# Expert stream of a fused attention, mixture-of-experts and HGRN layer: its first late piece and its last piece in two halves, its spare piece earlier, and a fourth pair of split-weight buffers in the second block

## The chip, the cores and the metric

One core of a Trainium2 chip runs the whole program. The metric is the device time of one execution in microseconds (us), median of several executions. TensorE is called PE below, VectorE DVE, ScalarE ACT, GpSimd POOL and SyncE SP; SP does nothing but wait on semaphores and issue transfers.

## The reference

The input is 256 tokens of width 1024 in float32. The first block is attention with a relative bias, a layer norm, and a mixture of 32 experts of which each token takes 4. The second block is an HGRN2 and convolution mixer and a gated feed-forward net of width 2816. The part around the change is the end of the first norm, the experts and the norm behind them, and then the matrix products of the second block.

```python
h = layer_norm(DEEPNORM_ALPHA * h + t, ln_g[i, 0], ln_b[i, 0])
f = moe_ffn(h, ...)
h = layer_norm(DEEPNORM_ALPHA * h + f, ln_g[i, 1], ln_b[i, 1])
...
logits = (xt @ w_router + b_router).astype(jnp.float32)
top_logit, top_e = lax.top_k(logits, TOP_K)
gate = jax.nn.softmax(top_logit, axis=-1)
...
def expert_block(args):
    h = xb @ w_gu[e] + b_gu[e]
    h_gate, h_up = jnp.split(h, 2, axis=-1)
    h_gate = jnp.minimum(h_gate, SWIGLU_LIMIT)
    h_up = jnp.clip(h_up, -SWIGLU_LIMIT, SWIGLU_LIMIT)
    act = h_gate * jax.nn.sigmoid(SWIGLU_ALPHA * h_gate) * (h_up + 1.0)
    return act @ w_down[e] + b_down[e]
```

## The kernel before

**The expert stream.** All weights of all 32 experts are read from HBM: per expert four pieces of `w_gu` and two of `w_down`, 2 MB each, 192 pieces numbered 0 to 191. They go to a ring of ten slots in SBUF; piece 10 (`SPARE`) alone has a place outside it, in the arena at 8192. Piece n of 11 and above goes to slot (n-1) mod 10, and SP issues its transfer (`load_piece`, L489) when `freed(n)` holds, which is that PE has finished with the piece that was in that slot: piece 11 waits for piece 0, piece 12 for piece 1, piece 15 for piece 4, piece 21 for piece 11, piece 22 for piece 12. The experts run in order, except that at the end the gate and up pieces of expert 31 come ahead of the down pieces of expert 30. So the last four pieces are 188 and 189 (down of expert 30) and 190 and 191 (down of expert 31).

**One expert on PE.** The tokens of the expert are gathered (L808, up to 64 of them), turned (L624), copied by ACT, multiplied with four gate and up pieces (L835), the result is clipped and gated on DVE and ACT, turned, multiplied with two down pieces (L843) and added to the sums of all tokens (`scatter`, L855). The bias of the expert is put into the accumulators first (`add_bias`, L827).

**Ahead of the stream.** Attention's output product (L751) ends tile by tile; DVE forms the sum, its norm with the rows `ln_g` and `ln_b` (`row_g`, `row_b`, arena 8192 to 10240) and so `h1`. PE turns `h1`, multiplies it with the router's weights (L790), DVE picks four experts a token (`choose`), PE counts the place of each token in its expert's list (L797 to L801), DVE makes the selection matrices, PE gathers. PE then makes three small tables of gates, places and counts (L624, L867), before the first expert starts. Since `row_g` and `row_b` lie where piece 10 goes, SP issues piece 10 only after `h1` of both tiles is done.

**Loads by POOL.** The rows of the first norm are loaded after the last row maximum, the small arrays of the router and of the gate biases after the last attention values; `bdown` and the rows of the second norm after piece 10 has been used.

**After the stream.** The last down result goes through ACT (`take_items`) and `scatter`, DVE and ACT form the norm of both tiles and the RMS norm of the second block. Its weights come in 1 MB pieces to six places in slots 3 to 5 (L545). ACT splits each piece into a high part (`split_hi`, L1198) and DVE into a low part (`split_lo`, L1552), in one of three pairs of buffers in slots 6 to 8 (`w_split`), and PE makes three products of them. The wait of `split_hi` is for PE to be done with the piece three before. In the last product (L1143) all accumulators are fed together for eight pieces, and then the last three are used once for each accumulator. Slot 9 is not used after the stream.

## Time and profile before

| | us |
|---|---|
| median of 3 runs | 1375.93 (1375.58 to 1377.43) |
| the profiled execution | 1376.69 |
| its span in the trace | 1374.9 |
| granted clock of PE, mean | 0.994 of full speed |
| attention and first norm, to the first expert product | 0 to 132.3 |
| expert stream, to the last down product | 132.3 to 1033.2 |
| second norm and second block | 1033.2 to 1374.9 |

The busy share of an engine says little here: PE counts as busy in 97% of the span, in all stages. What bounds a stage is read from what PE waits for in it, and from the rate of the transfers.

### The profile page before, as it was taken

The page shows a single profiled execution, that of the slowest core. Times are in us where ns is not written, and L with a number is a line of the kernel's source. Part 1 is how long each engine was busy: PE and PEld are TensorE (multiplying, and loading weights), DVE is VectorE, ACT ScalarE, POOL GpSimd, SP SyncE. Part 2 cuts the span into 40 slices and gives each one's busy share as a digit, 9 for nine tenths or more (in the row PEclk, how much of TensorE's full clock was granted, in tenths as well). Part 3 has the DMA queues.
Part 4 walks back from the last instruction along what each step waited for, and adds up shares of the span by engine and source line. Part 5 has one row for each costly group of instructions (what it writes and reads, how often), then busy time and mean ns, then how long its engine had stood idle before and what let it go on. Part 6 is the DMA issues. An engine that isn't in the chain of part 4 may idle for free.

```text
span 1374.9 us, 17056 instructions
## 1 busy us (share of the span) xinstructions
PE 1330.1 (97%) x7358; PEld 718.6 (52%) x7358; DVE 441.2 (32%) x746; ACT 346.9 (25%) x576; POOL 49.6 (4%) x60
## 2 busy tenths in 40 slices
PE   9999999999999999969999999999999999999997
PEld 7996333333333333323333333333336998999986
DVE  5565121112111111101211111111107776888854
ACT  4541011101101110100110101100116545666642
POOL 2010000000000000000000000000002000022200
PEclk9999999999999999989999999999999999999999
DMA  9968999999999999999999999999996444265530
GB/s 378 376 233 359 428 421 430 430 432 429 430 431 430 430 431 429 431 429 430 431 432 429 432 429 431 429 431 430 432 427 242 153 154 153 87 254 183 184 123 31
DMA packets 44378, 484.17 MB, mean 352 GB/s; under 512 B 4780, under 2 KB 4832, under 8 KB 13712
## 3 DMA queue, kind: packets, MB, share of 16 engines
q1 hardware_dynamic: 42432, 477.63, 83.4%
q0 software_dynamic: 1872, 5.44, 1.1%
q8 instruction: 59, 0.97, 0.3%
q14 instruction: 15, 0.12, 0.0%
HBM read 481.99 MB, written 1.06 MB: 351 GB/s over the span
## 4 chain that ended last, share of the span: by engine, by line
PE 78%; DMA 15%; DVE 4%; issue 1%; ACT 1%; DVEq 0%; SPq 0%; ACTq 0%
PE bank L835 25%; PE bank L641 19%; PE bank L843 13%; DMA ring<-in_moe_w_gate_up 12%; PE bank L1143 4%; PE bank L855 3%; PE bank L808 3%; PE bank L624 3%; DMA ring<-in_w_in 2%; PE bank L827 2%; PE bank L751 2%; PE bank L1079 1%; PE bank L1029 1%; DMA arena<-in_x_by_feature 1%; DVE w_split L1552 1%
## 5 line engine op out<-in xcount | busy, mean ns | idle before, releaser
L835 PE MATMUL bank<-ring,arena 128*64 128x512 f32 x2048 | 448.9, 594 | 9.8 <-DMA ring<-in_moe_w_gate_up 9.8
L835 PEld LDWEIGHTS bank<-ring,arena 128*64 128x64 f32 x2048 | 143.2, 137 | 313.2 <-issue 290.3
L1750 DVE TENSOR_SCALAR arena<-bank 128x512 f32<-128x512 f32 x32 | 22.1, 692 | 654.8 <-PE bank L835 654.7
L843 PE MATMUL bank<-ring,arena 128*64 128x512 f32 x1008 | 223.5, 595 | 1.8 <-DMA ring<-in_moe_w_down 1.3
L641 PE MATMUL bank<-x_hi,w_split 128*128 128x256 f32 x1056 | 195.2, 285 | 2.1 <-DVE x_lo L1559 2.1
L641 PEld LDWEIGHTS bank<-x_hi,w_split 128*128 128x128 f32 x1056 | 167.2, 193 | 2.6 <-DVE x_lo L1559 1.5
L1552 DVE TENSOR_TENSOR w_split<-ring,w_split 128x2048 fp32r<-128x2048 f32 x61 | 139.5, 2289 | 60.4 <-ACT w_split L1198 60.2
L641 PE MATMUL bank<-x_lo,w_split 128*128 128x256 f32 x528 | 150.1, 284 | 0.0
L1299 ACT ACTIVATE arena<-arena 128x512 f32<-128x512 f32 x32 | 20.2, 630 | 495.3 <-DVE arena L1750 495.3
L843 PEld LDWEIGHTS bank<-ring,arena 128*64 128x64 f32 x1008 | 69.8, 137 | 135.3 <-issue 126.4
L1198 ACT CAST w_split<-ring 128x2048 fp32r<-128x2048 f32 x62 | 118.2, 1910 | 74.2 <-PE bank L641 42.5
L641 PEld LDWEIGHTS bank<-x_lo,w_split 128*128 128x128 f32 x528 | 102.1, 193 | 0.0
L808 PE MATMUL bank<-arena 128*64 128x512 f32 x256 | 61.9, 605 | 10.6 <-issue 10.6
L1291 ACT COPY arena<-bank 128x512 f32<-128x512 f32 x32 | 18.7, 585 | 200.4 <-PE bank L843 200.4
L855 PE MATMUL bank<-arena 64*128 64x512 f32 x256 | 63.6, 615 | 1.5 <-ACT arena L1291 1.5
L624 PEld LDWEIGHTS bank<-cst,arena 128*128 128x128 f32 (+1 forms) x374 | 45.0, 188 | 34.9 <-DVE arena L1758 26.3
L624 PE MATMUL bank<-cst,arena 128*128 128x128 f32 (+1 forms) x374 | 54.4, 290 | 5.4 <-DVE arena L1758 3.3
L1143 PE MATMUL bank<-w_split,a_hi 128*128 128x512 f32 x176 | 54.4, 390 | 1.6 <-DVE w_split L1552 1.6
L2043 DVE SCALAR_TENSOR_TENSOR ring<-ring,vcol 128x256 f32<-128x256 f32 x88 | 48.8, 594 | 1.6 <-ACT ring L1526 0.8
L641 PE MATMUL bank<-w_split,x_hi 128*128 128x256 f32 x256 | 49.0, 287 | 0.0
L855 PEld LDWEIGHTS bank<-arena 64*128 64x128 f32 x256 | 22.0, 186 | 42.1 <-issue 38.6
L808 PEld LDWEIGHTS bank<-arena 128*64 128x64 f32 x256 | 18.4, 139 | 47.7 <-issue 46.9
(288 smaller groups left out, 1102.1 us busy)
## 6 DMA issues: line engine op xcount, KB each, us to landing
ring<-in_moe_w_gate_up SPq DMA_DIRECT2D x128, 2048.0 KB, 34.5
ring<-in_moe_w_down SPq DMA_DIRECT2D x63, 2048.0 KB, 34.1
ring<-in_ffn_w_up SPq DMA_DIRECT2D x22, 1024.0 KB, 4.8
ring<-in_w_in SPq DMA_DIRECT2D x14, 1024.0 KB, 8.0
ring<-in_ffn_w_down SPq DMA_DIRECT2D x11, 1024.0 KB, 4.9
ring<-in_a_w_in SPq DMA_DIRECT2D x10, 1024.0 KB, 20.9
ring<-in_a_w_out SPq DMA_DIRECT2D x2, 2048.0 KB, 14.0
ring<-in_w_out SPq DMA_DIRECT2D x4, 1024.0 KB, 5.0
```

What stands on the lines that cost most here:

```text
L624: return pe.transpose(dst, src, ident[0:rows, 0:rows])
L641: last = mm(dst[:, j * T:(j + 1) * T], lhs, rhs, start=c == 0 and n == 0, stop=c == KC - 1 and n == 2)
L751: last = mm(bank[OUT_BANKS[2 * g + t]][:, :], a, w[:, cols], start=h == 2 * first and k == 0, stop=h == 2 * last_q + 1 and k == 2)
L808: last = mm(bank[2][half * 64:half * 64 + 64, :], sel[:, t, :], h1[:, t, half * 512:(half + 1) * 512], start=t == 0, stop=t == NT - 1)
L827: mm(bank[q][half * 64:half * 64 + 64, :], bias_sel[rows, :], bgu[rows, :], start=True, stop=False)
L835: last = mm(bank[q // 2][half * 64:half * 64 + 64, :], chunk(xeT, c), w[:, c % 2, q * 512:(q + 1) * 512], start=False, stop=c == KC - 1)
L843: last = mm(bank[3][half * 64:half * 64 + 64, :], chunk(actT, c), w[:, c % 4, half * 512:(half + 1) * 512], start=c == 0, stop=c == KC - 1)
L855: last = mm(bank[4 + 2 * half + t][:, :], selgT[rows, t, :], y_item[rows, :], start=first, stop=True, skip_group_check=True)
L1143: last = mm(bank[2 * t + g][:, :], x, w, start=c == 0 and k == 0, stop=c == FB - 1 and k == 2)
L1198: copy(like(w_hi, p), pieces[p][2]).then_inc(hi_ready, 1)
L1552: tt(like(w_lo, p), pieces[p][2], like(w_hi, p).bitcast(f32), ALU.subtract).then_inc(lo_ready, 1)
L2043: last = stt(y[:, g, :], u[:, g, j:j + T], vcol[:, col:col + 1], y[:, g, :], ALU.mult, ALU.add)
```

## The change

1. The rows of the first norm get places of their own (`row_g0` at 13612, loaded early; `row_b0` at 6144, loaded when the attention values are done). Piece 10 is issued right then, ahead of pieces 0, 6, 7 and 8.
2. Piece 11 is loaded in two halves: the first when PE has done the first half of piece 0 (`first_chunk`), the second when it has done all of it.
3. The rows of the second norm are loaded by SP behind piece 191, and no longer by POOL after piece 10.
4. `h1` of each tile is announced in halves. Ranks, places and selection are made tile by tile, and the gather of the first tile runs ahead of the choice for the second. The first expert's bias is added earlier, and the three small tables are made behind piece 0. PE runs short fill products (`fill`) between them.
5. Piece 191 is loaded in halves, and PE uses each when it is there. `scatter(1)` and the turn of the gates of expert 31 move behind piece 190. ACT takes the last result ahead of `split_hi(IN2)`, and loads its table earlier.
6. From `IN2` on there are four pairs of split buffers; the fourth is slot 9. `split_hi` waits for the piece four before. Where ACT and DVE stand in their own order with each split is not changed.

```diff
+        row_g0, row_b0 = at(13612, D), at(6144, D)
...
         def arrived(n):
-            return ring_in[home(n)], 16 * sum(home(k) == home(n) for k in range(n + 1))
+            return ring_in[home(n)], 16 * sum((home(k) == home(n)) * (1 + (k == HALVED[0])) for k in range(n + 1))
+        HALVED = (SPARE + 1, N_EXP * PIECES_E - 1)
+        def split_of(p):
+            return p % SPLITS if p < IN2 else (p - IN2) % LATE_SPLITS
...
+            sp.wait_ge(o_ps, PAIRS)
+            load_piece(SPARE)
             for k, q in enumerate(OUT_ORDER):
                 sp.wait_ge(*((out_used, k + 1) if k < PAIRS - 1 else (out_ps, NT + 1)))
                 load_piece(SPLIT_X if q == SPLITS else SPLIT_FIRST + (OUT1 + q) % SPLITS)
-            sp.wait_ge(h1_ready, NT)
-            load_piece(SPARE)
-            for n in range(SPARE + 1, first_late):
+            sp.wait_ge(first_chunk, 1)
+            load_half(HALVED[0], 0)
+            sp.wait_ge(*freed(HALVED[0]))
+            load_half(HALVED[0], 1)
+            for n in range(SPARE + 2, first_late):
                 sp.wait_ge(*freed(n))
                 load_piece(n)
...
+            sp.wait_ge(*freed(HALVED[1]))
+            for j in range(2):
+                load_half(HALVED[1], j)
+            sp.dma_start(row_g, row(ln_g[1, :], D)).then_inc(ln1_in, 16)
+            sp.dma_start(row_b, row(ln_b[1, :], D)).then_inc(ln1_in, 16)
...
-            pool.wait_ge(max_ready, H)
-            pool.dma_start(row_g, row(ln_g[0, :], D)).then_inc(ln0_in, 16)
-            pool.dma_start(row_b, row(ln_b[0, :], D)).then_inc(ln0_in, 16)
+            pool.dma_start(row_g0, row(ln_g[0, :], D)).then_inc(rel_in, 16)
             pool.wait_ge(pt_ps, H)
             pool.wait_ge(o_ps, PAIRS)
+            pool.dma_start(row_b0, row(ln_b[0, :], D)).then_inc(ln0_in, 16)
...
             pool.dma_start(bdown, b_down[:, :]).then_inc(moe_small_in, 16)
-            pool.dma_start(row_g, row(ln_g[1, :], D)).then_inc(ln1_in, 16)
-            pool.dma_start(row_b, row(ln_b[1, :], D)).then_inc(ln1_in, 16)
...
+            pe.wait_ge(sel_ready, 1)
+            gather_first(0)
+            mm(RANKS[1], ones, chosen[:, 0, :], start=True, stop=False)
+            fill()
             pe.wait_ge(chosen_ready, 2)
-            mm(bank[0][:, N_EXP:2 * N_EXP], before, chosen[:, 1, :], start=False, stop=True).then_inc(rank_ps, 1)
-            repeat(3, 1)
+            mm(RANKS[1], before, chosen[:, 1, :], start=False, stop=True).then_inc(rank_ps, 1)
+            fill()
+            pe.wait_ge(sel_ready, 2)
+            gather_first(1).then_inc(xe_ps, 1)
+            fill()
...
+                    if n == 0:
+                        gate_up(s, buffer_of(n, 2), (0,)).then_inc(first_chunk, 1)
+                        gate_up(s, buffer_of(n, 2), (1,)).then_inc(piece_done, 1)
+                        tables()
...
+                    if n == HALVED[1]:
+                        scatter(1)
+                        pe.wait_ge(selg_ready, i + 1)
+                        turn_gates().then_inc(selgT_ps, 1)
+                        pe.wait_ge(*arrived(n))
+                        down_e(s, buffer_of(n, 4), (0, 1))
+                        pe.wait_ge(last_half_in, 32)
+                        down_e(s, buffer_of(n, 4), (2, 3)).then_inc(piece_done, 1)
...
-                elif p >= DOWN + SPLITS:
-                    act.wait_ge(piece_used, p - DOWN - SPLITS + 1)
+                elif p >= DOWN + LATE_SPLITS:
+                    act.wait_ge(piece_used, p - DOWN - LATE_SPLITS + 1)
...
                 if i == LAST:
-                    split_hi(IN2)
+                    nc.scalar.preload_act_table_set(log_exp)
                 if i != LAST - 1:
                     take_items(i)
+                if i == LAST:
+                    split_hi(IN2)
```

SP's order at the start of the stream, before: `in_moe_w_down` to the arena is piece 10, the ring piece behind it piece 11.

```order
L489 DMA ring<-in_moe_w_gate_up 128x4096
L489 DMA ring<-in_moe_w_down 128x4096
L489 DMA arena<-in_moe_w_down 128x4096
L489 DMA ring<-in_moe_w_down 128x4096
L489 DMA ring<-in_moe_w_gate_up 128x4096 x4
```

And of the change, with its waits at the same place:

```order
L500 DMA ring<-in_moe_w_down 128x4096 [waits lo_ready]
L500 DMA arena<-in_moe_w_down 128x4096 [waits o_ps]
L500 DMA ring<-in_moe_w_gate_up 128x4096 [waits out_used] x3
L500 DMA ring<-in_moe_w_gate_up 128x4096 [waits out_ps]
L510 DMA ring<-in_moe_w_down 128x2048 [waits first_chunk]
L510 DMA ring<-in_moe_w_down 128x2048 [waits piece_done]
L500 DMA ring<-in_moe_w_gate_up 128x4096 [waits piece_done] x4
```

Piece 10 now stands ahead of the four pieces that wait for the output product, and piece 11 is two rows.

PE's order from the ranks of the second tile to the end of the first expert's gate and up product, before (128x32 rows on L797 to L801 are ranks, L808 the gather, L624 turns, L867 counts, L827 the bias, L835 gate and up):

```order
L797 MATMUL bank<-arena,cst 128x32
L798 MATMUL bank<-arena,cst 128x32
L649 MATMUL bank<-cst 128x512
L801 MATMUL bank<-arena,cst 128x32
L649 MATMUL bank<-cst 128x512
L808 MATMUL bank<-arena 64x512 x4
L624 MATMUL bank<-cst,arena 32x128 x4
L867 MATMUL bank<-cst,arena 32x1 x2
L624 MATMUL bank<-cst,arena 128x128 x4
L827 MATMUL bank<-arena 64x512 x4
L835 MATMUL bank<-ring,arena 64x512 x32
```

And of the change, from the gather of the first tile (L814 gathers, L820 is a fill, L881 gate and up):

```order
L814 MATMUL bank<-arena 64x512 x2
L848 MATMUL bank<-arena,cst 128x32
L820 MATMUL bank<-cst 128x256
L851 MATMUL bank<-arena,cst 128x32
L820 MATMUL bank<-cst 128x256
L814 MATMUL bank<-arena 64x512 x2
L820 MATMUL bank<-cst 128x256
L650 MATMUL bank<-cst,arena 128x128 x4
L820 MATMUL bank<-cst 128x256
L881 MATMUL bank<-ring,arena 64x512 x8
L650 MATMUL bank<-cst,arena 32x128 x4
L917 MATMUL bank<-cst,arena 32x1 x2
```

Behind the last rank there is now half a gather where a whole one was, the bias is gone from there (it follows the first tile's router product), and the tables stand behind the eight products of piece 0.

## Rows read from the trace of the kernel before

**Rows 1.** The page: span, and the rate of transfers in 40 slices.
```profile
span 1374.9 us, 17056 instructions
GB/s 378 376 233 359 428 421 430 430 432 429 430 431 430 430 431 429 431 429 430 431 432 429 432 429 431 429 431 430 432 427 242 153 154 153 87 254 183 184 123 31
```
**Rows 2.** PE's waits, 135 to 1047 us: total us, times, longest.
```profile
PE bank L808 <- issue: 10.6, 1, 10.6
PE bank L835 <- DMA ring<-in_moe_w_gate_up: 9.8, 11, 1.5
...
PE bank L843 <- DMA ring<-in_moe_w_down: 1.3, 2, 1.1
```
**Rows 3.** Windows: busy by engine, PE clock, DMA share, GB/s.
```profile
108.00:112.00 4.00, 4.00 (x19) 3.32 (x18) 3.83 (x8) 0.41 (x2) 0.00 (x0) 1.00 0.06 19
200.00:250.00 50.00, 50.00 (x246) 17.40 (x244) 7.10 (x16) 6.30 (x12) 0.00 (x0) 1.00 1.01 430
```
**Rows 4.** Timeline of SP's queue: issues of pieces 11, 12 and 21.
```profile
135.97 0.33 SPq L489 DMA_DIRECT2D ring<-in_moe_w_down  x1
139.41 0.33 SPq L489 DMA_DIRECT2D ring<-in_moe_w_gate_up  x1
...
186.48 0.33 SPq L489 DMA_DIRECT2D ring<-in_moe_w_gate_up  x1
```
**Rows 5.** DMA issues to landing: alone at 77.17, pieces 11, 12, 21, second norm's `ln_b`.
```profile
ring<-in_moe_w_gate_up SPq DMA_DIRECT2D x1, 2048.0 KB, 7.8
...
ring<-in_moe_w_down SPq DMA_DIRECT2D x1, 2048.0 KB, 8.8
...
ring<-in_moe_w_gate_up SPq DMA_DIRECT2D x1, 2048.0 KB, 10.2
...
ring<-in_moe_w_gate_up SPq DMA_DIRECT2D x1, 2048.0 KB, 10.6
...
arena<-in_ln_b POOLq DMA_DIRECT2D x1, 512.0 KB, 13.3
```
**Rows 6.** Timeline, all engines, 127 to 133 us.
```profile
127.96 1.94 PE L808 MATMUL bank<-arena 128*64 128x512 f32 x8
...
129.83 0.61 PE L624 MATMUL bank<-cst,arena 128*32 128x128 f32 x4
...
130.59 0.74 PE L624 MATMUL bank<-cst,arena 128*128 128x128 f32 x4
...
131.26 1.09 PE L827 MATMUL bank<-arena 32*64 32x512 f32 x8
...
131.37 0.58 ACT L1296 COPY arena<-bank 128x512 f32<-128x512 f32 x1 [0.84 <-PE bank L624]
...
132.28 7.95 PE L835 MATMUL bank<-ring,arena 128*64 128x512 f32 x36
```
**Rows 7.** Timeline, all engines, 1019 to 1039 us.
```profile
1019.50 3.65 PE L843 MATMUL bank<-ring,arena 128*64 128x512 f32 x16 [1.09 <-DMA ring<-in_moe_w_down]
...
1026.13 7.09 PE L843 MATMUL bank<-ring,arena 128*64 128x512 f32 x32
...
1031.61 1.90 ACT L1198 CAST w_split<-ring 128x2048 fp32r<-128x2048 f32 x1 [5.00 <-DMA ring<-in_w_in]
...
1035.29 1.29 DVE L1817 BATCH_NORM_STATS2 arena<-bank 128x6 f32<-128x512 f32 x2 [17.95 <-PE bank L855]
...
1036.08 0.60 ACT L1349 ACTIVATE arena<-bank 128x512 f32<-128x512 f32 x1 [0.79 <-PE bank L855]
...
1038.37 0.21 DVE L1823 TENSOR_SCALAR arena<-arena 128x1 f32<-128x1 f32 x1
```
**Rows 8.** Timeline, second block: where PE or ACT waited at a split.
```profile
1162.37 0.73 PE L1079 MATMUL bank<-w_split,x_hi 128*128 128x512 f32 x2 [0.18 <-DVE w_split L1552]
...
1350.33 1.91 ACT L1198 CAST w_split<-ring 128x2048 fp32r<-128x2048 f32 x1 [3.53 <-PE bank L1143]
...
1354.62 0.73 PE L1143 MATMUL bank<-w_split,a_hi 128*128 128x512 f32 x2 [1.61 <-DVE w_split L1552]
```

More of the change, by code:

```diff
@@ L775, in _, with add_bias, gather_first, fill @@
             before = const("before")
+            def add_bias():
+                for half in range(2):
+                    for q in range(2):
+                        rows = slice((half * 2 + q) * 32, (half * 2 + q) * 32 + 32)
+                        mm(bank[q][half * 64:half * 64 + 64, :], bias_sel[rows, :], bgu[rows, :],
+                           start=True, stop=False)
+            def gather_first(t):
+                for half in range(2):
+                    last = mm(bank[2][half * 64:half * 64 + 64, :], sel[:, t, :], h1[:, t, half * 512:(half + 1) * 512],
+                              start=t == 0, stop=t == NT - 1)
+                return last
+            def fill():
+                mm(bank[3][:, 0:T], ident, cst[:, 0:T], start=True, stop=True)
             for t in range(NT):
-                pe.wait_ge(h1_ready, t + 1)
                 for g in range(2):
+                    pe.wait_ge(h1_ready, 2 * t + g + 1)
                     b = 4 + 2 * t + g
@@ L928, in _ @@
                     pe.wait_ge(y_ready, LAST)
-                    for t in range(NT):
-                        scatter(t)
+                    scatter(0)
                 if i + 1 < N_EXP and not pause:
```

151 lines of the change are left out of this document (82 added, 69 removed).

## The prediction

> **What bounds the kernel now.** I read the page first, for the rate of transfers in its 40 slices, then what PE waits for in the expert stream, then the windows around the start of the stream, then SP's issues with their times to landing, and last the timelines at both ends of the stream and in the second block.
>
> The page [rows 1] shows three stages. From the fifth slice to the 30th, the transfers run at about 430 GB/s without a gap; that is the expert stream. Before it there are dips, and after it the rate falls to half. In the stream PE waits for transfers 13 times, 11.1 us in all (9.8 and 1.3) [rows 2]; the 10.6 us wait between experts is its own, at the point where it looks for extra items, and the transfers run on beneath it. So in the stream PE has 11.1 us to spare and the transfers have none: the DMA share of a window is 1.01 at 430 GB/s [rows 3], and one piece (2.097 MB) takes 4.88 us. The stream ends earlier only if the pieces come earlier. Behind it the second block is bound by PE.
>
> **How early the pieces can come** has two sides.
>
> The supply side is how long the transfers stand idle before the stream, and what else they carry. From 108 to 112 us their share is 0.06 [rows 3]: SP has issued all that it may and waits for the output product. That is a hole of 3.8 us.
>
> The demand side is when a slot comes free. SP issues piece n when PE has used the piece that was in its slot. A piece that is issued alone lands 7.8 us later, one issued into a queue lands later than that [rows 5]. What it takes over 7.8 us is how much earlier the transfers could have been free for it without running dry. I call it the margin. It is 1.0 us for piece 11 (8.8 - 7.8), 2.4 for piece 12 (10.2 - 7.8) and 2.8 for piece 21 (10.6 - 7.8) [rows 5], which were issued at 135.97, 139.41 and 186.48 us [rows 4]. From there on they grow: PE takes 900.9 us for 32 experts [rows 6, 7], less its waits of 21.7 [rows 2], 27.5 each, and the transfers need 6 x 4.88 = 29.3. The start decides.
>
> **The change part by part.**
>
> Piece 10 goes out when the attention values are done, near 99 us, and fills the hole. It takes 4.88 us, the hole gives 3.8, and `row_b0` (0.5 MB, 1.2 us at the same rate) is now carried there too. The four pieces behind start late by what doesn't fit, so the supply gains 2.6 to 3.8 us. `row_g0` is loaded at 27 us beside attention's weights and nothing waits for it.
>
> The rows of the second norm are 1.05 MB, 2.4 us of transfer, which the stream carried between its pieces 20 and 21 and now does not. Supply gains 5.0 to 6.2 us in all.
>
> Demand moves with PE. The first expert's product starts at 132.28 us [rows 6]. Ahead of it stand the gather (1.94 us from 127.96), the turn (130.59), ACT's copy (131.37 to 131.95) and the bias, which ends last (131.26 + 1.09 = 132.35). Now half the gather is done before (0.97 less), the bias too (0.3 less, since the copy is then last), and PE comes to the last rank up to 0.15 us late because a fill stands before it. The product starts 1.1 us earlier. The tables, from 129.83 to the turn at 130.59 [rows 6], take 0.76 us and now stand behind piece 0. So piece 0 is used 1.1 us earlier and everything behind it 0.35, and I take 0.4.
>
> Now the margins decide. Piece 11 is no limit: its first half is issued after the first half of piece 0, some 3.4 us before the old 135.97. Piece 12 allows 2.4 + 0.4 = 2.8 us, which is all that the hole gives. Piece 21 allows 2.8 + 0.4 = 3.2, and there the 2.4 us of the norm's rows come on top of 2.8, which makes 5.2. Two of these run into a slot that isn't free, and the queue runs dry for about 2 us near 187. **The stream gains 3.2 us**, not 5 to 6. From below, if the gain of 0.4 were a loss of 1, it is 1.8; from above, with the supply as the only limit, 6.2.
>
> At this place a rule of the Trainium skill gives another margin. The row has 7.8 us for a piece that is issued alone [rows 5]. The page "DMA: Bandwidth & Descriptors", section "Anatomy of one DMA", has a fixed 2.0 us plus the bytes at 436 GB/s, 6.8 us for a piece, as an estimate from its figures. By it each margin is 1.0 us larger, the stream gains 4.2, and the whole 6.0. The same rule would charge 2.0 us for each added half if the transfers ran one after another; the 4.88 us a piece in the stream says that a queue hides it.
>
> PE then waits 11.1 - (3.2 - 0.4) = 8.3 us in the stream, still well above nothing, so the whole 3.2 us reach its end.
>
> The end of the stream: PE last waits at piece 189, until 1019.50 us, and then works without a pause to 1033.22 (1026.13 + 7.09) [rows 7]. Piece 191 lands two pieces behind 189, near 1029.3, and is begun at 1029.7. Its half comes earlier than anyone needs it; `scatter(1)` and the gates only change places. All work from 189 on is PE's, and I cost this edit at nothing (0.2 us either way). What hides it is PE's own 13.7 us from 1019.50; without that, the half would be worth one half of a down product, 1.8 us. ACT's cast of the first `w_in` piece ends at 1033.51, hard against the copy of the last result, so putting it behind gives 0.1 at most.
>
> The rows of the second norm now stand behind piece 191 in SP's queue. Counted in the old times, `w_in` landed at 1031.6 [rows 7] and piece 191 2.4 us before. The rows land by 1031.6, and DVE needs them at 1035.29 [rows 7]. `w_in` lands at 1034.0, its cast ends at 1035.9, and ACT's next work starts at 1036.08 [rows 7]. Cost nothing, with 0.2 us to spare there and about 1 more before DVE's mean at 1038.37 would be late.
>
> The fourth pair of buffers: `split_hi` of the last `ffn_w_down` piece waits for the piece three before and starts at 1350.33 after 3.53 us of idling; PE then stands 1.61 us at 1354.62 [rows 8]. The wait for the piece four before ends one round of the product earlier, 5.4 us (3.53 + 1.91), so the 1.61 go. The 0.18 at 1162.37 [rows 8] goes too. Elsewhere in the second block PE doesn't wait at a split, and the splits keep their place on ACT and DVE, so nothing more can come. **1.8 us**, from 0 to 1.8.
>
> **The sum**: 3.2 + 0 + 1.8 = 5.0 us off the profiled execution, whose span is 1374.9 us [rows 1] and time 1376.69: 1369.9 and 1371.7. The median of the runs shown lies 0.8 below the profiled one, so the median should be **1370.9 us**. What a measurement of this kernel can tell from no change is about 0.2%, 2.75 us.
>
> **The rivals.**
>
> *Supply decides* (0.12). If the slots are free in time after all, the stream gains 3.8 + 2.4 = 6.2 us, the whole 8.0: 1367.9. For it: the margin is a difference of landings, and the landing of a single piece may hold slack. Against it: the margin of piece 11 is only 1.0 us, and the queue was full there without any dip.
>
> *PE starts late* (0.20). `row_b0` now stands ahead of the router's weights and the gate biases in POOL's queue, and piece 10 runs beside them. When `ln_b` stood behind another row in mid-stream it took 13.3 us to land [rows 5]. The router's product has slack of about 7 us there. If it is used up, or DVE waits for `row_b0`, PE starts at its old time and piece 12 is used 0.8 us late: the stream gains 2.0, the whole 3.8, 1372.1; with another microsecond 1373.1.
>
> *The norm's rows hold up the second block* (0.06), the one that ends slower. They stand in front of `w_in` in SP's queue, and ACT waits for `w_in` ahead of the norm's sums. If the two rows took what `ln_b` did in mid-stream, 13.3 us instead of 2.4, ACT would start the sums 10.9 us later less the 0.2 to spare: 1370.9 + 10.7 = 1381.6. The point from which it eats the gain of 5.0 is rows that take about 7.6 us (2.4 + 0.2 + 5.0). Against it: then the queue carried expert pieces too, and here it does not.
>
> *The split buffers give nothing* (0.07). ACT and DVE keep their order, and if something else in it holds back the last split, the sum is 3.2: 1372.7.
>
> **How the numbers follow.** The forecast has 0.55, with 1370.0 to 1372.0 as its own range. The range 1369.0 to 1373.4 takes in the late start, the missing split gain and the rule's 6.0 us, and leaves out the full supply and the slow rows. Faster by over 0.2% is below 1373.2: the forecast, full supply, no split gain and most of the late start, 0.80 after a discount for what I have not seen. Within 0.2% 0.14, slower 0.06.
>
> **What would show it.** In the profile after, piece 10 is issued near 100 us and the window 108 to 112 carries 400 GB/s. The first expert's product starts near 131.2. Pieces 12 and 21 land about 8 us after their issue, which means dry, and a dip stands near 187. PE waits for pieces 8 us instead of 11. The last down product ends near 1030.0. PE has no wait at a split near 1350. The forecast is wrong if piece 21 still has a margin (then more was to be had), if the first expert starts at 132 or later, or if ACT's first sum of the norm waits for `w_in`.

## The result, and the profile after

| | before | changed |
|---|---|---|
| median | 1375.58 us (1375.36 to 1377.43, 5 runs) | 1381.88 us (1381.75 to 1387.45, 5 runs) |
| span of the profiled execution | 1374.9 us | 1380.0 us |
| first expert product begins | 132.28 | 138.93 |
| piece 189 begins on PE | 1019.50 | 1026.43 |
| first product of the second block | 1049.91 | 1058.90 |
| last product ends | 1368.76 | 1373.92 |

The change makes the kernel slower: ratio 1.0053, 95% interval 1.0036 to 1.007. The prediction had 1370.9 us and 0.06 for slower.

The page of the changed kernel, span and transfers in 40 slices, to be held against [rows 1]:

```profile
span 1380.0 us, 17073 instructions
GB/s 375 391 204 371 344 395 430 430 431 430 430 431 430 431 432 430 431 430 431 429 432 430 430 431 431 430 429 432 430 428 298 163 127 179 64 273 184 184 122 31
```

The hole of the fourth slice has become smaller (359 to 371), as meant. But the fifth and sixth slices (138 to 206 us) fell from 428 and 421 to 344 and 395. The next view is PE's timeline ahead of the first expert:

```profile
121.98 3.61 PE L838 MATMUL bank<-arena 128*128 128x32 f32 x16 [4.42 <-DMA arena<-in_moe_b_gate_up]
125.51 1.99 PE L808 MATMUL bank<-arena 32*64 32x512 f32 x8
...
130.90 1.97 PE L838 MATMUL bank<-arena 128*128 128x32 f32 x16 [0.64 <-DVE arena L1760]
```

The router's product (L838) stood ready at 117.56 (the end of the fill product ahead of it) and waited 4.42 us for the biases of the gates; before the change it began at 117.18. What follows is slow too: its 16 rows take 3.61 us, where those of the second tile take 1.97, and `add_bias` (L808) takes 1.99. The windows say why (columns as in [rows 3]; the last line is the kernel before at the place of the third):

```profile
108.00:112.00 4.00, 4.00 (x19) 3.33 (x18) 2.09 (x6) 0.41 (x2) 0.00 (x0) 1.00 1.03 423
122.00:128.00 6.00, 6.00 (x25) 4.25 (x26) 1.54 (x8) 0.00 (x0) 0.00 (x0) 0.50 1.01 431
134.00:142.00 8.00, 7.57 (x36) 3.18 (x35) 1.79 (x8) 2.46 (x3) 0.00 (x0) 1.00 0.26 100
180.00:200.00 20.00, 20.00 (x106) 7.67 (x104) 4.03 (x13) 3.15 (x6) 0.50 (x1) 1.00 0.95 388
...
134.00:142.00 8.00, 8.00 (x40) 2.73 (x38) 0.00 (x0) 0.00 (x0) 0.00 (x0) 1.00 1.01 420
```

The first is the hole of 3.8 us, filled. In the second PE's granted clock is 0.50, so 1.2 GHz of 2.4. The low clock is not peculiar to this execution: the mean granted clock of the five timed ones is 0.986 to 0.992. The third is a new hole: all ten slots and the arena are full, and SP waits for PE to use piece 0 (it issues the first half of piece 11 at 140.90). So 423 GB/s at 108 us are paid back by 100 GB/s at 134 to 142 us.

The small loads behind this are in the list of DMA issues of 99 to 105 us (size, median us to landing), and the row behind the dots is that of the last bias alone, issued at about 103.95. Before the change the same biases landed after 6.8 us in the median and 7.3 for the last (the line at the end), the router's weights after 8.0:

```profile
arena<-in_moe_w_down SPq DMA_DIRECT2D x1, 2048.0 KB, 17.3
arena<-in_ln_b POOLq DMA_DIRECT2D x1, 512.0 KB, 11.6
arena<-in_moe_b_gate_up POOLq DMA_DIRECT2D x4, 64.0 KB, 13.7
arena<-in_moe_w_router POOLq DMA_DIRECT2D x1, 128.0 KB, 12.8
...
arena<-in_moe_b_gate_up POOLq DMA_DIRECT2D x1, 64.0 KB, 18.0
...
arena<-in_moe_b_gate_up POOLq DMA_DIRECT2D x1, 64.0 KB, 7.3
```

103.95 and 18.0 make 121.95, which is when PE goes on.

At the other end, the timeline of 1026 to 1059 us (it answers to [rows 7]; the last two lines are the kernel before):

```profile
1026.43 3.65 PE L889 MATMUL bank<-ring,arena 128*64 128x512 f32 x16 [1.07 <-DMA ring<-in_moe_w_down]
1031.83 3.65 PE L889 MATMUL bank<-ring,arena 128*64 128x512 f32 x16
1036.84 3.65 PE L889 MATMUL bank<-ring,arena 128*64 128x512 f32 x16
1042.42 1.30 DVE L1886 BATCH_NORM_STATS2 arena<-bank 128x6 f32<-128x512 f32 x2 [17.82 <-PE bank L901]
1043.15 4.52 POOL L622 TENSOR_TENSOR w_split<-ring,w_split 128x2048 fp32r<-128x2048 f32 x1 [851.79 <-ACT w_split L1260]
1045.64 2.05 DVE L1702 SCALAR_TENSOR_TENSOR arena<-arena 128x1 f32<-128x1 f32 x1
1051.00 0.22 DVE L1702 SCALAR_TENSOR_TENSOR arena<-arena 128x1 f32<-128x1 f32 x1
...
1033.59 4.50 POOL L596 TENSOR_TENSOR w_split<-ring,w_split 128x2048 fp32r<-128x2048 f32 x1 [848.71 <-ACT w_split L1198]
1038.50 0.21 DVE L1640 SCALAR_TENSOR_TENSOR arena<-arena 128x1 f32<-128x1 f32 x1
```

DVE's operation on one column takes 2.05 us the first time and 0.22 the second. The first ends at 1047.69, and POOL's subtraction at 1047.67. Before the change POOL was done (1038.09) when DVE came to this operation (1038.50).

**The balance.** By the two traces: the first product is 6.65 us later, the stream adds 0.28 (6.93 at piece 189), the new order of its last products 0.34 (last down product at +7.27), the meeting of POOL and DVE 1.72 (first product of the second block at +8.99). Then 1.50 come back because the clock stood at 1.00 where before the change it had been 0.52 and 0.63 (216 products in 26.18 us, not 27.68), and 0.45 in the middle of the block, of which 0.18 is the wait at 1162.37 [rows 8] that is gone; the rest was not looked into. The fourth pair gives 1.88 (the down product begins at +7.04, the last one ends at +5.16). The 1.50 are no work of the change: the clock of the kernel before, at 1050 to 1052 us, is

```profile
1050.00:1052.00 2.00, 2.00 (x10) 2.00 (x11) 2.00 (x6) 2.00 (x4) 0.00 (x0) 0.52 0.90 309
```

and some other versions show it low there and some don't (see the last section).

### The profile page after: what moved, and what is told of

Same layout as the page of the kernel before. It is cut to its first block, busy times and chain, and to the rows that moved or that the text cites. A ratio compares the mean times of both kernels' runs of the same rounds, so it can differ in the third digit from the quotient of the medians.

```text
span 1380.0 us, 17073 instructions
## 1 busy us (share of the span) xinstructions
PE 1334.8 (97%) x7362; PEld 720.4 (52%) x7362; DVE 443.7 (32%) x750; ACT 346.8 (25%) x576; POOL 48.6 (4%) x58
## 3 DMA queue, kind: packets, MB, share of 16 engines
HBM read 481.99 MB, written 1.06 MB: 350 GB/s over the span
## 4 chain that ended last, share of the span: by engine, by line
PE 84%; DMA 11%; DVE 3%; issue 1%; ACT 1%; POOL 0%; SPq 0%; DVEq 0%; POOLq 0%
PE bank L881 27%; PE bank L667 18%; PE bank L889 15%; DMA ring<-in_moe_w_gate_up 6%; PE bank L1205 4%; PE bank L901 4%; PE bank L861 3%; PE bank L650 3%; DMA ring<-in_moe_w_down 3%; PE bank L808 2%; PE bank L1141 2%; DMA arena<-in_moe_b_gate_up 1%; PE bank L1091 1%; DMA arena<-in_x_by_feature 1%; PE bank L1153 1%
## 5 line engine op out<-in xcount | busy, mean ns | idle before, releaser
L881 PE MATMUL bank<-ring,arena 128*64 128x512 f32 x2048 | 449.8, 595 | 7.4 <-DMA ring<-in_moe_w_gate_up 7.1
L881 PEld LDWEIGHTS bank<-ring,arena 128*64 128x64 f32 x2048 | 143.5, 137 | 311.0 <-issue 294.6
L667 PE MATMUL bank<-x_hi,w_split 128*128 128x256 f32 x832 | 154.2, 284 | 2.1 <-DVE x_lo L1621 2.1
L1361 ACT ACTIVATE arena<-arena 128x512 f32<-128x512 f32 x32 | 20.2, 630 | 494.8 <-DVE arena L1819 494.8
L667 PEld LDWEIGHTS bank<-x_hi,w_split 128*128 128x128 f32 x832 | 131.4, 192 | 2.6 <-DVE x_lo L1621 1.5
L1614 DVE TENSOR_TENSOR w_split<-ring,w_split 128x2048 fp32r<-128x2048 f32 x49 | 112.0, 2290 | 44.4 <-ACT w_split L1260 44.3
L667 PE MATMUL bank<-x_lo,w_split 128*128 128x256 f32 x416 | 117.7, 283 | 0.0
L1260 ACT CAST w_split<-ring 128x2048 fp32r<-128x2048 f32 x50 | 95.3, 1907 | 46.7 <-PE bank L667 31.8
L667 PEld LDWEIGHTS bank<-x_lo,w_split 128*128 128x128 f32 x416 | 79.8, 192 | 0.0
L667 PE MATMUL bank<-w_split,x_hi 128*128 128x256 f32 x224 | 43.1, 287 | 0.0
L667 PE MATMUL bank<-x_hi,w_split_late 128*128 128x256 f32 x224 | 41.7, 283 | 0.0
```

The source lines that it names most:

```text
L667: last = mm(dst[:, j * T:(j + 1) * T], lhs, rhs, start=c == 0 and n == 0, stop=c == KC - 1 and n == 2)
L881: last = mm(bank[q // 2][half * 64:half * 64 + 64, :], chunk(xeT, c), w[:, c % 2, q * 512:(q + 1) * 512], start=False, stop=c == KC - 1)
L1260: copy(like(w_hi, p), pieces[p][2]).then_inc(hi_ready, 1)
L1614: tt(like(w_lo, p), pieces[p][2], like(w_hi, p).bitcast(f32), ALU.subtract).then_inc(lo_ready, 1)
```

## The experiments

Each was timed against the kernel before on the same chip; the ratios are to that. "The early-bias version" is the first experiment's.

**1. Gate biases early.** The changed kernel, with the four loads of the gate biases moved on POOL to stand behind `row_g0`, near 28 us.

```diff
             pool.dma_start(row_g0, row(ln_g[0, :], D)).then_inc(rel_in, 16)
+            for half in range(2):
+                for q in range(2):
+                    r = half * 2 + q
+                    pool.dma_start(bgu[r * 32:(r + 1) * 32, :], b_gu[:, q * 1024 + half * 512:q * 1024 + half * 512 + 512]
+                                   ).then_inc(moe_small_in, 16)
```

The same lines are taken out behind the load of `br`.

> The changed kernel with one edit: the four loads of the gate biases (64 KB each) are issued by POOL near 28 us, right behind row_g0, and no longer behind row_b0 and the router's weights near 102 us. Theory (small loads that share the transfer engines with piece 10 land late, PE waits 4.4 us at L838, its clock falls to half, and so every slot of the ring comes free 7.5 us late): the wait at L838 falls under 1 us, the clock stays at 1.00, the first expert product starts near 131.5 us instead of 138.9, and the time falls from 1381.9 to about 1375. If the margins of the prediction (2.4 and 2.8 us) hold as well, 1373. Rival (the new order on PE and DVE, with fills and tables, is what is slow): the first product stays behind 136 us and the time above 1380.

Measured: 1373.56 us, ratio 0.9993 (0.9984 to 1.0002). The wait is gone, the clock is 1.00 in all windows of 112 to 142 us, the first product begins at 131.33. This one move is worth 8.3 us by the medians and undoes the loss. But piece 189 begins at 1018.10, only 1.40 us ahead of before, where the prediction had 3.2. The time is near the 1373 that was expected if the margins held, and they did not: 1.50 us of the gain in this execution are the clock near 1050 us, which stood at 1.00. First product and windows:

```profile
131.33 3.65 PE L881 MATMUL bank<-ring,arena 128*64 128x512 f32 x16 [0.24 <-ACT arena L1358]
...
134.00:142.00 8.00, 8.00 (x44) 2.81 (x42) 2.06 (x8) 0.00 (x0) 0.00 (x0) 1.00 0.94 318
180.00:200.00 20.00, 20.00 (x98) 6.44 (x96) 0.00 (x0) 0.61 (x2) 0.52 (x1) 1.00 0.94 371
200.00:250.00 50.00, 50.00 (x246) 17.42 (x242) 7.10 (x16) 6.31 (x12) 0.00 (x0) 1.00 1.01 431
```

At 180 to 200 us the transfers run at 371 GB/s, though pieces 21 and 22 took 10.1 and 10.5 us to land, well above the 7.8 that I had taken as the mark of a dry queue.

**2. Piece 10 late again.** The changed kernel, with SP waiting for the router's small loads ahead of piece 10.

```diff
-            sp.wait_ge(o_ps, PAIRS)
+            sp.wait_ge(moe_small_in, 6 * 16)
             load_piece(SPARE)
```

> The changed kernel with one edit: SP issues piece 10 only when all six small loads of the router have landed, instead of with the attention values. Its place in SP's order is the same. Theory (piece 10 beside the small loads delays them): they land within 9 us of their issue, near 112 us, PE does not wait for them, the first product starts near 131.5, and the time is about 1376; the hole of 108 to 112 us is back. Rival (row_b0, which now stands ahead of them in POOL's queue, delays them by itself): they land after 117 us, a wait of 2 us or more stays at L838, and the time is 1379 or more.

Measured: 1375.71 us, ratio 1.0 (0.9991 to 1.0009). Piece 10 goes out at 112.03, the biases land after 7.0 to 8.2 us, with `row_b0` still ahead of them, and PE doesn't wait. The first product begins at 131.16, piece 189 at 1018.17. So without piece 10 beside them the small loads are in time, even with `row_b0` ahead of them. And filling the hole is worth 0.07 us at piece 189 (1018.17 against 1018.10), or 0.24 counted from each version's own first product: less than one execution of each can tell from nothing, and far from the prediction's 2.8. The median lies 2.2 above that of experiment 1 all the same; in the profiled execution the clock was 0.50 at 1050 to 1054 us, where it was 1.00 in experiment 1, and the two fastest executions (1372.95 and 1373.05) are as fast as the fastest there (1373.12).

**3. The fourth pair alone**, on the kernel before.

```diff
+LATE_SPLITS = 4
...
+        w_split_late = sb("w_split_late", [P, 2, HALF], (SPLIT_FIRST + SPLITS) * SLOT, f32r)
...
-                elif p >= DOWN + SPLITS:
-                    act.wait_ge(piece_used, p - DOWN - SPLITS + 1)
+                elif p >= DOWN + LATE_SPLITS:
+                    act.wait_ge(piece_used, p - DOWN - LATE_SPLITS + 1)
```

> The kernel before with part 6 of the change alone: the fourth pair of split buffers. The profile after has the last PE work 1.9 us nearer to the start of the down product than before. Theory: that is this part's and nothing else's, so the time is 1.8 to 2.0 us below before, about 1373.8. Rival (it came from the shift of the whole second block): 1375.6, and PE still waits 1.6 us at L1143.

Measured: 1374.38 us, ratio 0.9984 (0.9975 to 0.9993), so 1.0 to 3.4 us faster. PE no longer waits at a split. The predicted 1.8 lies in it.

**4. Order at the end of the stream**, on the early-bias version: ACT casts the first `w_in` piece ahead of its copy of the last down result, and the rows of the second norm go behind that piece.

```diff
-            sp.dma_start(row_g, row(ln_g[1, :], D)).then_inc(ln1_in, 16)
-            sp.dma_start(row_b, row(ln_b[1, :], D)).then_inc(ln1_in, 16)
...
+                if pos == 0:
+                    sp.dma_start(row_g, row(ln_g[1, :], D)).then_inc(ln1_in, 16)
+                    sp.dma_start(row_b, row(ln_b[1, :], D)).then_inc(ln1_in, 16)
...
                 if i == LAST:
                     nc.scalar.preload_act_table_set(log_exp)
+                    split_hi(IN2)
                 if i != LAST - 1:
                     take_items(i)
-                if i == LAST:
-                    split_hi(IN2)
```

> The edit of e1_bias_early, and at the end of the stream ACT casts the first w_in piece ahead of the last result again, and SP issues the two rows of the second norm behind the first w_in piece instead of ahead of it. Theory (the cast's late place makes POOL's 4.5 us subtraction run into DVE's norm, where a 0.2 us DVE operation took 2.05 us until POOL was done): POOL ends before DVE's refinement, that operation takes 0.2 us, and the time is 2.0 us below e1_bias_early. Rival (that operation was slow for another reason): it is slow here too, and the time is that of e1_bias_early within 0.3 us.

Measured: 1373.88 us, ratio 0.9979 (0.997 to 0.9988). DVE's operation takes 0.21 us, and POOL is done (1039.19) when it begins (1039.70). From the begin of piece 189 to the first product of the second block pass 30.61 us, against 32.48 in the early-bias version and 30.41 before the change. So POOL's subtraction behind a late cast had cost 1.9 us. (Two edits were made at once, but no engine waits for the rows in either version.) In the profiled execution the clock was 0.50 at 126 to 132 us, the first product came at 133.67, 2.34 late, and piece 189 at 1020.50, 2.40 late. No wait of PE over 0.27 us stood in the 10 us ahead of that.

**5. More pieces in halves**, on the early-bias version: 12 to 23 as well.

```diff
+        FIRST_HALVED = range(HALVED[0], 24)
...
-            sp.wait_ge(first_chunk, 1)
-            load_half(HALVED[0], 0)
-            sp.wait_ge(*freed(HALVED[0]))
-            load_half(HALVED[0], 1)
-            for n in range(SPARE + 2, first_late):
+            for n in FIRST_HALVED:
+                sp.wait_ge(first_chunk, freed(n)[1])
+                load_half(n, 0)
+                sp.wait_ge(*freed(n))
+                load_half(n, 1)
```

PE announces the half of each piece up to the one whose slot piece 23 takes, in its gate and up and in its down products.

> The version with the gate biases early, and besides pieces 12 to 23 loaded in halves as piece 11 is: the first half is issued when PE has done one half of the piece in its slot, some 1.7 us before the second. Theory A, the stream is tied to PE (its end follows the first expert product by 887 us, because the early transfers are asked for too late to keep the queue full): the dip of the transfers at 134 to 140 us and those near 187 and 192 us become smaller, PE's waits for pieces fall below 9.0 us, and piece 189 begins 1 to 2.5 us earlier than the 1018.10 of that version. Theory B, the stream's length is that of its transfers, 29.3 us an expert, once it runs: the end moves by less than 0.3 us, or comes later by what halves of 1 MB lose in rate.

Measured: 1373.31 us, ratio 0.9978 (0.9969 to 0.9987). The first product begins at 131.22 as before, but piece 189 at 1016.58, 1.5 us earlier; PE's waits for pieces fall from 10.1 to 7.0 us. The same bytes, half of each piece asked for about 1.8 us earlier (piece 12 at 137.54, not 139.37), brought the end of the stream forward. So in the early stream the rate of the transfers was not the limit, the time of the requests was.

**6. The norm's rows in the stream again**, on the early-bias version.

```diff
             pool.dma_start(bdown, b_down[:, :]).then_inc(moe_small_in, 16)
+            pool.dma_start(row_g, row(ln_g[1, :], D)).then_inc(ln1_in, 16)
+            pool.dma_start(row_b, row(ln_b[1, :], D)).then_inc(ln1_in, 16)
```

> The version with the gate biases early, with the rows of the second norm back on POOL behind bdown, where they stood before (piece 10 used), and not behind piece 191. Theory A (the early pieces are asked for too late, so the transfers have idle time near 187 us in any case): the rows fill idle time in part; piece 189 begins at most 1.0 us later than 1018.10. Theory B (supply): 2.4 us later, 1020.5. In both the first cast of w_in no longer stands behind the rows.

Measured: 1376.66 us, ratio 1.0002 (0.9993 to 1.0011). Piece 189 begins at 1018.87, 0.77 us later than 1018.10 and 1.1 later counted from its own first product at 130.99. By these numbers more than half of the rows' 2.4 us of transfer fell into time in which the transfers would have idled; the table below shows how far one execution can be trusted here. The window 180 to 190 us is full again, 402 GB/s.

**7. POOL's subtraction in quarters**, on the early-bias version.

```diff
-            pool.tensor_tensor(like(w_lo, IN2), pieces[IN2][2], like(w_hi, IN2).bitcast(f32), ALU.subtract
-                               ).then_inc(lo_ready, 1)
+            for j in range(4):
+                part = slice(2 * j, 2 * j + 2)
+                last = pool.tensor_tensor(like(w_lo, IN2)[:, part, :], pieces[IN2][2][:, part, :],
+                                          like(w_hi, IN2)[:, part, :].bitcast(f32), ALU.subtract)
+            last.then_inc(lo_ready, 1)
```

> The version with the gate biases early, with POOL's subtraction for the first w_in piece (4.53 us, 1034.83 to 1039.36) cut in four parts of about 1.15 us. There DVE's 128x1 refinement took 1.99 us instead of 0.2 and ended with POOL's subtraction. Theory A: a DVE operation of this form can't begin while a POOL operation runs; it then ends with the quarter in progress, takes 0.3 to 1.3 us, and the norm is 0.7 to 1.7 us earlier. Theory B: it shares a port throughout, or waits for something else at that place: it still takes about 2 us.

Measured: 1375.52 us, ratio 0.9996 (0.9987 to 1.0005). The timeline of DVE, and POOL's row:

```profile
1035.47 1.40 DVE L1873 SCALAR_TENSOR_TENSOR arena<-bank,arena 128x512 f32<-128x512 f32 x2
1036.91 0.21 DVE L1895 TENSOR_SCALAR arena<-arena 128x1 f32<-128x1 f32 x1
1037.04 1.28 DVE L1705 SCALAR_TENSOR_TENSOR arena<-arena 128x1 f32<-128x1 f32 x1
1038.35 0.15 DVE L1709 TENSOR_SCALAR arena<-arena 128x1 f32<-128x1 f32 x1
1038.54 1.00 DVE L1710 TENSOR_TENSOR arena<-arena 128x1 f32<-128x1 f32 x1
...
1034.57 4.96 POOL L624 TENSOR_TENSOR w_split<-ring,w_split 128x512 fp32r<-128x512 f32 x4 [850.96 <-ACT w_split L1263]
```

The quarters are 1.24 us each and end near 1038.29 and 1039.53. The first held operation ends at 1038.32, the next of its kind at 1039.54. So DVE gets in between two POOL operations and is held again by the next: 1.9 us in all (1.06 and 0.84), as with one piece. Theory A had the first operation right and missed the second. Not held are the operations with one input, and L1873, whose other input is in a bank. The Trainium skill has this in "SBUF — State Buffer", section "SBUF: two separate sides": VectorE and GpSimd share a pair of ports as an exclusive lock for a whole instruction, and a VectorE operation with two inputs in SBUF needs it against a GpSimd operation that reads SBUF. The traces agree, and also with its other half, that a GpSimd operation which only writes doesn't hold it. In the kernel before, two DVE operations of that form with 512 columns ran beside POOL's memsets in 1.42 us, and their like took 1.40 with POOL idle:

```profile
1038.62 1.86 POOL L602 MEMSET ring<- 128x1024 f32 x2
...
1039.13 1.42 DVE L1807 SCALAR_TENSOR_TENSOR arena<-arena 128x512 f32<-128x512 f32 x2
...
1042.79 1.40 DVE L1807 SCALAR_TENSOR_TENSOR arena<-arena 128x512 f32<-128x512 f32 x2
```

**8. `row_b0` behind the gate biases**, in the changed kernel.

```diff
-            pool.dma_start(row_b0, row(ln_b[0, :], D)).then_inc(ln0_in, 16)
             pool.dma_start(wr, w_router.rearrange("(c p) e -> p c e", p=P)).then_inc(moe_small_in, 16)
...
+            pool.dma_start(row_b0, row(ln_b[0, :], D)).then_inc(ln0_in, 16)
```

> The changed kernel with one edit: POOL issues row_b0 behind the router's weights and the gate biases instead of ahead of them. Piece 10 runs beside them as before. Theory A, it is piece 10 that slows them: they take 10 to 14 us to land as in the changed kernel (median 13.7) and the last lands less than 2 us earlier than there; row_b0 lands later, DVE waits for it 3 to 6 us, and the whole is no faster than the changed kernel. Theory B, it is row_b0 ahead of them in their own queue: they land in 7 to 9 us, as before the change.

Measured: 1384.41 us, one execution, so its time is not compared and only its trace is read. The last bias took 14.6 us to land, against 18.0 in the changed kernel and 7.3 before the change; it came at about 117.9, 4.1 earlier than in the changed kernel. The row took 20.2, and DVE waited 14.19 us for it.

```profile
arena<-in_moe_b_gate_up POOLq DMA_DIRECT2D x1, 64.0 KB, 14.6
```

So neither theory has it alone: with the row moved away the landing is still double that of before, which is piece 10, and the row ahead of the biases adds 3.4 us and 0.7 of later issue. It adds them only beside piece 10 (in experiment 2 the biases landed after at most 8.2 us behind the row). The price then only moves to the row.

**9. All parts together**: experiments 4 and 5 in one kernel.

> The version with pieces 11 to 23 in halves and the gate biases early, and besides the two edits at the end of the stream: ACT casts the first w_in piece ahead of its copy of the last down result, and the rows of the second norm go behind that piece instead of ahead of it. Theory: DVE's refinement no longer meets POOL's subtraction (0.2 us instead of 2.0), so the first product of the second block stands about 30.6 us behind the begin of piece 189 instead of 32.5, and the median is 1.5 to 2.0 us below that version's, 0.33 to 0.38% below the kernel before. Rival: the rows land too late now that the stream ends earlier, DVE waits for them, and nothing is gained.

Measured: 1370.71 us, ratio 0.9962 (0.9949 to 0.9976): 0.38% faster than before, the lowest median of all. It is near the predicted 1370.9, but by edits that the prediction did not have. From piece 189 to the second block 30.62 us. Its five executions lie in two groups, 1370.0 to 1370.7 (mean granted clock 0.994 to 0.995) and 1374.3 to 1374.5 (0.992 to 0.993). The profiled one is of the second, and its windows show a low clock at two places:

```profile
126.00:128.00 2.00, 2.00 (x6) 0.39 (x6) 1.50 (x8) 0.32 (x1) 0.00 (x0) 0.50 1.01 434
...
132.00:140.00 8.00, 7.70 (x40) 3.13 (x40) 0.89 (x5) 2.46 (x3) 0.00 (x0) 1.00 0.59 212
...
1050.00:1052.00 2.00, 1.97 (x10) 1.97 (x11) 2.00 (x6) 2.00 (x5) 0.00 (x0) 0.55 0.74 264
```

The clock fell at 125 us, with no wait over 0.27 us in the 9 us ahead of it, and at 1050 us; the first product begins at 134.49.

**10. Fills at the norm**: the same with 7 more fill products (128x512, made by `repeat`) in the gaps at 1044 to 1050 us.

```diff
             pe.wait_ge(x2_ready, 2)
-            repeat(3, 3)
+            repeat(3, 6)
...
+            repeat(7, 2)
             pe.wait_ge(xn_ready, 2)
...
+            repeat(7, 2)
```

> The version with all parts, and 7 more fill products of PE (3 ahead of the turns of the normed tiles, 2 between the tiles, 2 behind), in the three gaps of 0.9 to 1.7 us at 1044 to 1050 us where PE waits for DVE. Theory A, PE's clock falls to half at about 1050 us in some executions because PE has idled there: the window 1048 to 1056 us shows 1.00, the group of 216 products takes 26.2 us, and the median is 0.5 to 1.5 us below the version with all parts, with less spread. Theory B, the drop isn't due to these gaps: the same median within 0.5 us, or later by up to 0.5 us where a fill stands in the way of a turn.

Measured: 1373.53 us, ratio 0.9984 (0.9975 to 0.9993). The windows at 1048 to 1056 us show 1.00, and 9 of 11 executions lie within 0.83 us (1373.39 to 1374.22). But a fill takes 0.87 to 0.94 us, not the 0.43 that I had reckoned: each is two rows of the trace. They stand in the way of the turns, and the second block begins 33.67 us behind piece 189, 3.05 later than in experiment 9. The gain of a steady clock is less than that. Whether the fills kept the clock up isn't settled, since experiments 1 and 7 show no drop there without them.

**11. PE late by fills**: the early-bias version with 5 fills ahead of the first expert product.

```diff
             fill()
+            repeat(3, 5)
```

> The version with the gate biases early, and 5 fill products of PE (0.43 us each, 2.1 us) between the turn of the first gather and the first expert product, partly under ACT's copy (0.8 us). The first product is 1.4 to 2.1 us later. Theory A, the stream is tied to PE's start: piece 189 begins later by the same 1.4 to 2.1 us. Theory B, transfers set the end, with PE's 9 us of waits as slack: it begins no later.

Measured: 1381.06 us, ratio 1.0029 (1.002 to 1.0038). The delay was 3.92 us (the fills again 0.87 each): first product at 135.25, piece 189 at 1023.13, 5.03 later. All of the delay arrives at the end, and 1.1 more.

**12. Fills in the wait**: the changed kernel with 10 more fills where PE idles for the biases.

```diff
-                    repeat(3, 1)
+                    repeat(3, 11)
                     pe.wait_ge(moe_small_in, 6 * 16)
```

> The changed kernel with 10 more fill products of PE (4.3 us) in the 4.4 us in which it idles for the gate biases at 117.6 to 122.0 us. Theory A, the idle time itself lowers PE's clock to 0.50, which costs as much again as the wait: the clock stays 1.00 there, the first expert product comes 2 to 2.5 us earlier than the 138.93 of the changed kernel, and the median is 2 to 2.5 us below its 1381.9. Theory B, the clock falls for another reason or costs nothing: no change beyond 0.5 us.

Measured: 1382.57 us, ratio 1.0045 (1.0029 to 1.006). The fills took 9.61 us and ended at 125.9, so they overran the wait by 3.8, and the size of the clock's share can't be read from this run. It tells something else:

```profile
116.31 9.61 PE L675 MATMUL bank<-cst 128*128 128x512 f32 x22
...
124.00:126.00 2.00, 2.00 (x8) 1.01 (x7) 0.00 (x0) 0.00 (x0) 0.00 (x0) 1.00 1.01 434
...
132.00:140.00 8.00, 8.00 (x30) 4.23 (x29) 2.73 (x14) 0.91 (x2) 0.00 (x0) 0.62 0.47 197
```

PE had worked since 116.31 us with no wait over 0.64, and its clock still fell, later. So a long wait is not needed for a fall, and experiments 4 and 9 say the same. That a wait plays no part isn't shown either: with the wait filled, the four executions have mean granted clocks of 0.993 to 0.996, against 0.986 to 0.992 in the changed kernel, and in experiment 8 the clock was 0.50 from 118 to 128 us, from inside PE's wait of 9.14 us on. What lowers the clock stays open.

**One table over all.** First expert product, begin of piece 189, and the difference:

| kernel | first product | piece 189 | us between |
|---|---|---|---|
| before | 132.28 | 1019.50 | 887.22 |
| changed | 138.93 | 1026.43 | 887.50 |
| 1 biases early | 131.33 | 1018.10 | 886.77 |
| 2 piece 10 late | 131.16 | 1018.17 | 887.01 |
| 3 fourth pair | 132.73 | 1020.12 | 887.39 |
| 4 cast and rows | 133.67 | 1020.50 | 886.83 |
| 5 more halves | 131.22 | 1016.58 | 885.36 |
| 6 rows in stream | 130.99 | 1018.87 | 887.88 |
| 7 quarters | 131.16 | 1017.83 | 886.67 |
| 8 row behind | 142.10 | 1028.99 | 886.89 |
| 9 all parts | 134.49 | 1019.41 | 884.92 |
| 10 fills at norm | 131.16 | 1017.34 | 886.18 |
| 11 PE late | 135.25 | 1023.13 | 887.88 |
| 12 fills in wait | 141.81 | 1027.77 | 885.96 |

The first product varies over 11.1 us, the difference over 3.0. The stream is tied to PE's start nearly one to one, although PE waits 7 to 10 us for pieces in it. How much one execution can vary is seen from versions with the same stream: 1, 4, 7 and 11 lie between 886.67 and 887.88, and those with more halves, 5, 9 and 10, between 884.92 and 886.18. The two sets don't overlap, so the earlier requests shorten the stream, by about 1.5 us in the mean. Experiment 12 reaches 885.96 without them, with the second latest start of PE; part of the spread is not explained. The 0.07 to 0.24 of experiment 2 and the 0.8 to 1.1 of experiment 6 are no larger than the 1.2 between equal streams, and say only that the first is well below the predicted 2.8 and the second probably below 2.4.

## Why the prediction was wrong

**Demand: "the product starts 1.1 us earlier".** It started 6.65 later. This is the failing step: the sum put the wait for the router's small loads at nothing. It was written down as a rival, *PE starts late*, with two errors in its size, and the prediction's own sign of being wrong, a first expert at 132 or later, came true. It had "slack of about 7 us", and that was right: before the change the last bias was issued at about 103.25 and landed 7.3 later, at 110.6, and the product began at 117.18 (6.6 later; against the 117.56 of the changed kernel 7.0). What failed is the landing. I took it from the 13.3 us that `ln_b` needed in mid-stream [rows 5], 6 more than 7.3 and so just inside the slack. Measured are 18.0: 7.3 more by piece 10 (14.6 in experiment 8) and 3.4 by the place behind `row_b0`; with 0.7 of later issue this is 11.4 against a slack of 7.0, which leaves the wait of 4.4. The second fault is the price, which I had capped at the old start and "another microsecond". The runs show 4.42 of waiting and then 3.2 at a low clock: the early-bias version needs 13.79 us from the router's product to the first expert product (117.54 to 131.33), the changed one 16.95 (121.98 to 138.93). With the loads in time both are gone in the profiled executions of experiments 1 and 2. Experiments 4 and 9 show a like low clock without late loads, so its cause stays open. With the cause gone (experiment 1) the product does start 0.95 us earlier. Experiment 2 shows piece 10 as the condition, experiment 8 the row's place as a second part; the prediction had named both.

**"Everything behind it 0.35, and I take 0.4".** In the early-bias version piece 12 is issued at 139.37 against 139.41 [rows 4], so 0.04. The first product is 0.95 earlier, but the first product of piece 1 stands 4.34 us behind it where it stood 3.43 behind: the tables cost 0.91, not 0.76.

**Supply: 5.0 to 6.2 us.** The bytes are as said; the hole is filled. They are worth little because the stream hangs on the requests. Experiment 2 gives 0.07 to 0.24 us for the hole, experiment 6 0.8 to 1.1 for the rows, both within the spread of one execution.

**The margins: 2.8 us at piece 21.** The idea was right, that the slot's release decides, and the size was wrong. The whole gain of the stream was 1.40 instead of 3.2, of which 0.95 is the earlier start. The mark of 7.8 us for "dry" is too low: at 10.1 to 10.5 us to landing the transfers were already down to 371 GB/s. The rule of the Trainium skill that I had weighed against it ("DMA: Bandwidth & Descriptors", "Anatomy of one DMA") gave still larger margins (a gain of 4.2), and the measurement speaks against it more than against the row. The page gives that fit for loads issued by GpSimd, and the pieces are issued by SP, which the prediction did not say.

**PE's waits: 8.3 us.** The changed kernel has 8.2 (7.1 and 1.1), by accident: its late start had given the transfers time. The early-bias version has 10.1 (9.0 and 1.1). That the number fits in the changed kernel is luck.

**End of the stream: nothing.** 0.34 us for the order of the last products, a little outside the 0.2 either way. But the later cast moved POOL's subtraction onto DVE's norm: 1.7 to 1.9 us. I had looked at what ACT and DVE wait for and not at what POOL does beside them; the prediction gave "0.1 at most" to the cast's move.

**The norm's rows behind piece 191: nothing**, and the rival with 10.7 us. No wait of DVE or ACT for the rows shows in any run, so that held. The rival's 1381.6 is almost the measured 1381.88, by coincidence: its mechanism did not occur.

**The fourth pair: 1.8 us.** It gave 1.88 in the changed kernel and 1.0 to 3.4 alone. Right in size and mechanism. ACT still waits 3.53 us ahead of its last split, but this split now stands 5.4 us nearer to the start (+1.59 against 1350.33, where PE is at +7.04), as predicted, and PE no longer waits for it:

```profile
1351.92 1.91 ACT L1260 CAST w_split<-ring 128x2048 fp32r<-128x2048 f32 x1 [3.53 <-PE bank L1205]
```

## What to carry to other kernels

A load that is moved forward into a hole of the transfers also runs beside everything issued there. List the small loads in flight, take from the trace when each landed and when its reader was ready, and allow for far more than the old time to landing before you call the hole free: here it went from 7.3 to 18.0 us.

A stream whose buffers are freed by its consumer can keep the consumer's start: here a microsecond lost ahead of the first piece arrived whole at the end (3.92 lost, 5.03 late in experiment 11), although the consumer waits for transfers later on. Before more supply, ask earlier, by halves of the first pieces.

When an operation moves, look at all four engines at its new time, and at POOL and DVE together.

## What had not been expected of the hardware

- Loads of 64 KB by POOL took 13.4 to 18.0 us to land beside two 2 MB loads by SP and behind a row of 512 KB, against 6.5 to 7.3 beside one 2 MB load and without the row. The second 2 MB load itself took 17.3.
- A one-column DVE operation with two inputs in SBUF took 1.00 to 2.06 us while a POOL subtraction ran, and 0.2 otherwise; cutting POOL's work in four changed nothing in the sum.
- PE's granted clock fell to 0.50 in some executions, for 3 to 10 us each time: between 117 and 141 us in six of the 14 profiled ones (changed, 3, 4, 8, 9, 12), and near 1050 us in eight, the kernel before among these. In 3, 4, 9 and 12 no wait over 0.8 us stood in the 9 us ahead of the first fall. It cost 0.5 us (experiment 3) to 3.2 us (changed) at the first place and 1.4 to 1.9 at the second. The times of one kernel spread with it: in experiment 1 the six executions with a mean clock of 0.995 or 0.996 took 1373.1 to 1373.6 us, the five with 0.989 to 0.993 took 1375.1 to 1377.4.
- A fill product of 128x512 in float32 takes 0.87 us at full clock and stands as two in the trace.
